# A fused block of five layers on one core: the first mixer begins with the pooling branch, contraction outermost, and the norm's affine part moves behind the spatial product

## What is computed

```python
mod = silu(c) @ ada_w[l] + ada_b[l]              # 1024 -> 3072
shift, scale, gate = jnp.split(mod, 3, axis=-1)
h = x * (1.0 + scale) + shift
proj = h @ w_in                                  # 1024 -> 5120
u, v, z_a, x_b, z_b = split(proj)                # 1024 each
# spatial unit: 4 heads of 256 features, blocks of 128 tokens
v = layer_norm(v per head, norm_g, norm_b)       # norm_g, norm_b: 256
sv = einsum('hts,bnshd->bnthd', masked ws, v) + bs.T
a = u * sv * silu(z_a)
# pooling: 4 groups of 256, trailing means over 2, 4, 8, 16 tokens, minus the token
y = einsum('bsgd,gde->bsge', pooled(x_b), pool_w)
b = (y + pool_b) * pool_scale * silu(z_b)
y = concat([a, b]) @ w_out
x = layer_norm(ALPHA * x + (1.0 + gate) * y, ln_g, ln_b)
```

## Time and profile before

| | |
|---|---|
| median of 3 runs | 1896.85 us (1893.95 to 1897.05) |
| profiled execution | 1895.36 us |
| its span, first to last instruction | 1893.6 us |
| PE busy | 1815.3 us, 96% |
| DVE, ACT, POOL busy | 819.3, 737.6, 832.9 us |
| mean granted clock of PE | 0.991 of full speed |
| output projection of the first mixer begins | 301.61 us |

### The profile page before, as it was taken

How to read it: one execution, slowest core, us unless ns; L and a number is a source line. 1 busy time by engine, 2 the same in 40 slices (tenths; PEclk the granted TensorE clock), 3 DMA queues, 4 the chain that set the end, 5 groups by cost and what they waited for, 6 DMA issues and landing times.

```text
span 1893.6 us, 24041 instructions
## 1 busy us (share of the span) xinstructions
PE 1815.3 (96%) x8796; PEld 1503.0 (79%) x8796; DVE 819.3 (43%) x1388; ACT 737.6 (39%) x1030; POOL 832.9 (44%) x1033
## 2 busy tenths in 40 slices
PE   5999899989999999899999999999997999999998
PEld 5887778877888878788888888888965788888886
DVE  7478666467767750733151111102678341111102
ACT  2223322265565651422253443313556354344222
POOL 1666565447010153255425555353444135555352
PEclk9999999999999999899999999999999999999999
DMA  9234645422121223134323334322311133333321
GB/s 309 89 112 126 190 162 179 161 63 59 36 72 38 79 100 111 46 91 131 99 80 89 106 93 122 111 89 89 116 57 45 45 90 89 92 108 89 109 102 67
DMA packets 211649, 191.19 MB, mean 101 GB/s; under 512 B 10504, under 2 KB 192891, under 8 KB 211579
## 3 DMA queue, kind: packets, MB, share of 16 engines
q1 hardware_dynamic: 210944, 189.95, 32.5%
q10 hardware_dynamic: 634, 0.29, 0.1%
HBM read 188.12 MB, written 2.10 MB: 100 GB/s over the span
## 4 chain that ended last, share of the span: by engine, by line
PE 85%; DVE 6%; ACT 3%; POOL 2%; issue 2%; DMA 1%; SPq 1%; ACTq 0%; POOLq 0%; DVEq 0%
PE PS L1710 26%; PE PS L1712 26%; PE PS L1711 26%; POOL w_low L610 2%; PE PS L2009 1%; PE PS L1838 1%; ACT w_high L706 1%; PE PS L2040 1%; SPq L436 1%; DVE ada_odd L1099 1%; DMA ada_raw<-in_ada_w 1%; POOL w_low L648 1%; DVE soft L1665 0%; DVE probs L1663 0%; PE PS L2032 0%
## 5 line engine op out<-in xcount | busy, mean ns | idle before, releaser
L610 POOL TENSOR_TENSOR w_low<-w_raw,w_high 128x256 fp32r<-128x256 f32 x949 | 741.7, 819 | 822.7 <-ACT w_high L706 822.6
L1710 PE MATMUL PS<-h_high,w_high 128*128 128x512 f32 (+1 forms) x1488 | 560.9, 377 | 17.0 <-DVE h_low L1343 7.1
L706 ACT ACTIVATE w_high<-w_raw 128x2048 fp32r<-128x2048 f32 (+1 forms) x150 | 281.9, 1880 | 729.1 <-PE PS L1712 693.4
L1711 PE MATMUL PS<-h_low,w_high 128*128 128x512 f32 (+1 forms) x1488 | 555.1, 373 | 0.0
L1712 PE MATMUL PS<-h_high,w_low 128*128 128x512 f32 (+1 forms) x1488 | 554.9, 373 | 0.0
L1710 PEld LDWEIGHTS PS<-h_high,w_high 128*128 128x128 f32 x1488 | 283.1, 190 | 69.4 <-DVE h_low L1343 8.3
L1712 PEld LDWEIGHTS PS<-h_high,w_low 128*128 128x128 f32 x1488 | 282.8, 190 | 48.9
L1711 PEld LDWEIGHTS PS<-h_low,w_high 128*128 128x128 f32 x1488 | 283.3, 190 | 45.7 <-issue 0.5
L1216 DVE TENSOR_TENSOR gate_buf<-gate_buf,PS 128x512 f32<-128x512 f32 x44 | 30.2, 688 | 335.5 <-ACT gate_buf L756 334.8
L1271 DVE TENSOR_TENSOR w_low<-w_raw,w_high 128x2048 fp32r<-128x2048 f32 x11 | 25.2, 2292 | 315.4 <-ACT w_high L706 315.4
L1710 PE MATMUL PS<-w_high,ff_high 128*128 128x512 f32 x352 | 137.3, 390 | 0.1
(11 more groups left out here) (302 smaller groups left out, 2612.4 us busy)
## 6 DMA issues: line engine op xcount, KB each, us to landing
w_raw<-in_f_gate_up SPq DMA_DIRECT2D x88, 512.0 KB, 4.9
w_raw<-in_e_w_in SPq DMA_DIRECT2D x40, 512.0 KB, 4.8
w_raw<-in_f_down SPq DMA_DIRECT2D x40, 512.0 KB, 4.2
gains<-in_ada_w SPq DMA_DIRECT2D x16, 1024.0 KB, 5.2
w_raw<-in_a_w_in SPq DMA_DIRECT2D x24, 512.0 KB, 4.4
w_raw<-in_o_w_in SPq DMA_DIRECT2D x20, 512.0 KB, 4.4
ada_raw<-in_ada_w SPq DMA_DIRECT2D x8, 1024.0 KB, 11.9
w_raw<-in_e_w_out SPq DMA_DIRECT2D x16, 512.0 KB, 6.4
```

The costliest lines, as they stand in the source:

```text
L610: ins = nc.gpsimd.tensor_tensor(WL[s][:, piece], raw[s][:, piece], WH[s][:, piece].bitcast(F32), ALU.subtract)
L706: nact(WH[s][:, 0:n], raw[s][:, 0:n], ACT.Copy).then_inc(w_high[s], 1)
L1710: mm(dst, lh, rh, start=first, stop=False, skip_group_check=True)
L1711: mm(dst, lh, rl, start=False, stop=False, skip_group_check=True)
```

## The change

- The ring's stages `v`, `xb`, `pool` and `zb` become one stage `front` of seven pairs in the order xb (five chunks), zb (four), v (four), pool (one). `zu` comes behind it, directly ahead of `eout`.
- xb's first seven column tiles are made with the contraction outermost: four chunks, each of two k tiles by seven column tiles (896 columns), into seven banks that stay open. The eighth column tile is a chunk of its own of 1024 columns.
- The modulation blocks are loaded and used in the order 0, 4, 1, 5, 2, 6, 3, 7, so that two blocks give shift and scale of two k tiles; after two blocks DVE makes these four columns. Blocks 2 to 7 are turned into columns between the matmuls of xb.
- x is transposed by feature tiles into banks 0 to 7; ACT evicts it, tiles 0 and 1 with scale and shift, the others as they are, and modulates them later from SBUF. DVE takes the low parts of h and of the first four weight chunks.
- The affine part of the norm is applied behind the spatial product: norm_g as a scale of the output's partitions, norm_b times the row sums of the masked weights (one more product, by a matrix of ones) in the bias.
- The pooling's rounding and low parts are done by groups, on ACT and DVE. Its product is evicted by ACT into `yb`, silu(z_b) is kept in `zs`, their product comes later (`pool_gate`).
- Positions 0 to 3 of the later modulation blocks are used up in `front`, 4 to 11 in `zu`.

The core of the diff:

```diff
 RING = [
-    ("v", 2, (2, 2)),
-    ("xb", 2, (2, 2)),
+    ("front", 7, (2, 2)),
     ("zu", 4, (2, 2)),
-    ("pool", 1, (2, 2)),
-    ("zb", 2, (2, 2)),
...
+ADA_ORDER = (0, 4, 1, 5, 2, 6, 3, 7)
+XB_TILES = 7
+XB_DEEP = XB_TILES * P
+FRONT_SIZE = [2 * XB_DEEP] * 4 + [K * P] + [CHUNK] * 9
+ZB_AT, V_AT, POOL_AT = 5, 9, 13
...
# SP
+            first_ada(0)
+            first_ada(1)
+            load_xb(0)
             for t in range(T):
                 sp.dma_start(x[:, t, :], ...)
+            for j in range(1, 4):
+                first_ada(2 * j)
+                first_ada(2 * j + 1)
+                load_xb(j)
...
+            load_zb(0)
+            sp.wait_ge(hx_low, K)
             ada_load(0)
+            load_zb(1)
+            ada_load(1)
+            load_zb(2)
+            load_zb(3)
+            ada_load(2)
+            load_v(0)
+            ada_load(3)
+            load_v(1)
+            ada_load(4)
+            load_v(2)
+            load_v(3)
...
+            for c in range(8):
                 load_zu(c)
+                if c >= 2:
+                    ada_load(c + 3)
+                if c == 3:
+                    sp.wait_ge(sv_ready, K)
+                    gate_load(0)
...
# ACT
+            for j in range(1, 4):
+                front_high(j)
+                modulated(2 * j)
+                modulated(2 * j + 1)
+            front_high(4)
+            front_high(ZB_AT)
...
+            for f in range(K):
+                xb_out(f)
+            front_high(ZB_AT + 1)
+            for q in range(4):
+                if q < 3:
+                    pooled_high(q)
+                zb_gate(q)
+                front_high(ZB_AT + 2 + q)
+            pooled_high(3)
+            front_high(V_AT + 2)
+            front_high(V_AT + 3)
+            v_root(0)
+            front_high(POOL_AT)
+            front_high(POOL_AT + 1)
+            for f in range(3):
+                pool_out(f)
+            v_root(1)
+            for f in range(3, K):
+                pool_out(f)
+            zb_high(0)
+            zb_high(1)
+            front_high(POOL_AT + 2)
+            for f in range(2, K):
+                zb_high(f)
...
# DVE
+            for j in range(4):
+                first_terms(2 * j)
+                first_terms(2 * j + 1)
+                split_low("front", j // 2, j % 2, FRONT_SIZE[j])
+                dve.wait_ge(ada_done, 2 * j + 2)
+                v.tensor_tensor(of_step(mod[:, 0:2 * K], j), of_step(PS[:, 7, 256:256 + 2 * K], j), ..., ALU.add).then_inc(mod_ready, 1)
+                for kt in (2 * j, 2 * j + 1):
+                    dve.wait_ge(hx_high, kt + 1)
+                    v.tensor_tensor(hL[:, kt, :], h_tmp[kt % 4], hH[:, kt, :].bitcast(F32), ALU.subtract).then_inc(hx_low, 1)
...
+            def spatial(f):
+                h, m = f // 2, f % 2
+                steps.link(v.scalar_tensor_tensor(sv_bias[m], ws_sum[:, h, :], b_col, bs_bc[:, h * P:(h + 1) * P], ALU.mult, ALU.add))
+                dve.wait_ge(sp_done, f + 1)
+                v.scalar_tensor_tensor(sv[:, f, :]..., PS[:, f, :]..., g_col, sv_bias[m]..., ALU.mult, ALU.add).then_inc(sv_ready, 1)
...
+            ada_terms(0)
+            dve.wait_ge(w_high[1], BASE["front"].split[1] + ZB_AT // 2 + 1)
+            h = CHUNK // 2
+            v.tensor_tensor(WL[1][:, 0:h], ...).then_inc(front_dve, 1)
+            pool_rows(0)
+            pool_rows(1)
+            ada_terms(1)
+            pool_rows(2)
+            pool_rows(3)
+            pooled_low(0)
+            rest_columns()
+            ada_terms(2)
+            pool_rows(4)
+            pool_rows(5)
+            pooled_low(1)
+            dve.wait_ge(sum_done, 1)
+            v.tensor_copy(ws_sum, ...).then_inc(ws_sums, 1)
+            pool_rows(6)
+            pool_rows(7)
+            ada_terms(3)
+            pooled_low(2)
+            pooled_low(3)
+            gate_norm(0)
+            gate_norm(1)
...
+            pool_gate(0)
+            for f in range(K):
+                spatial(f)
+            for f in range(2, K, 2):
+                pool_gate(f)
...
# PE
+            first_column(0)
+            first_column(1)
...
+            for kt in range(K):
+                j, s = kt // 2, kt // 2 % 2
+                if kt % 2 == 0:
+                    front_split(j)
+                pe.wait_ge(hx_low, kt + 1)
+                for f in range(XB_TILES):
+                    if kt == 0:
+                        pe.wait_ge(xt_free, f + 1)
+                    c = slice((kt % 2) * XB_DEEP + f * P, (kt % 2) * XB_DEEP + (f + 1) * P)
+                    ins = mm3(PS[:, f, :], WH[s][:, c], WL[s][:, c], hH[:, kt, :], hL[:, kt, :], kt == 0, kt == K - 1)
...
+                    if kt % 2 and f == 3 and kt < K - 1:
+                        first_column(kt + 2)
+                if kt % 2 == 0 and kt < K - 2:
...
+                    first_column(kt + 2)
```

More of the change, by code:

```diff
@@ L592, in _ @@
             pool.sem_inc(ada_sum, CREDIT)
+            for first_layer in (tr_done, h_high, h_ready, mod_half):
+                pool.sem_inc(first_layer, T)
             def turn_queries(g):
@@ new lines, in _, with xb_out @@
+            front_high(0)
+            modulated(0)
+            modulated(1)
+            for kt in range(2, K):
+                x_turned(kt)
+            for j in range(1, 4):
[4 more added lines that the diff above has]
+            front_high(ZB_AT)
+            def xb_out(f):
+                if f < XB_TILES - 1:
+                    act.wait_ge(xb_done, f + 1)
+                elif f == XB_TILES - 1:
+                    act.wait_ge(used[1], BASE["front"].use[1] + 2)
+                else:
+                    act.wait_ge(used[0], BASE["front"].use[0] + 3)
+                nact(xbufs[f][:, PAD:], PS[:, f, :], ACT.Copy).then_inc(xb_ready, 1)
@@ new lines, in zb_gate, with pooled_high, v_root @@
+            def zb_gate(q):
+                s = (ZB_AT + q) % 2
+                act.wait_ge(used[s], BASE["front"].use[s] + (ZB_AT + q) // 2 + 1)
+                for m in range(2):
+                    nact(zs[:, 2 * q + m, :], PS[:, 2 * (q % 2) + m, :], ACT.Silu).then_inc(zs_ready, 1)
+            def pooled_high(g):
+                act.wait_ge(pooled_ready, 2 * g + 2)
+                nact(poolH[:, 2 * g:2 * g + 2, :], pooled[:, 2 * g:2 * g + 2, :], ACT.Copy).then_inc(pool_high, 1)
+            def v_root(n):
@@ L1130, in low_mod @@
                                 ALU.subtract).then_inc(h_ready, 1)
[L1132 to L1149 removed]
+            v.memset(ones[:, :], 1.0).then_inc(ones_ready, 1)
@@ new lines, in _, with pool_rows @@
+            for z in (*xbufs, sum_a, sum_b):
+                ins = v.memset(z[:, 0:PAD], 0.0)
+            steps.link(ins)
+            def pool_rows(f):
+                g = f // 2
+                win = POOL_WINDOWS[g]
+                dve.wait_ge(xb_ready, f + 1)
+                cur, step, nxt = xbufs[f], 1, [sum_a, sum_b]
+                while step < win:
+                    dst = nxt[0]
+                    nxt.reverse()
+                    steps.link(v.tensor_tensor(dst[:, PAD:], cur[:, PAD:], cur[:, PAD - step:PAD + S - step], ALU.add))
+                    cur, step = dst, 2 * step
+                steps.link(v.scalar_tensor_tensor(pooled[:, f, :], cur[:, PAD:], 1.0 / win, xbufs[f][:, PAD:], ALU.mult, ALU.subtract))
+                head = pooled[:, f, 0:PAD]
+                steps.link(v.tensor_tensor(head, cur[:, PAD:2 * PAD], inv_count[:, g * PAD:(g + 1) * PAD], ALU.mult))
+                v.tensor_tensor(head, head, xbufs[f][:, PAD:2 * PAD], ALU.subtract).then_inc(pooled_ready, 1)
@@ L1876, in _ @@
                     ins.then_inc(ws_tr, 1)
-                pe.wait_ge(w_split[s], B.split[s] + n + 1)
+                if q == 1:
+                    pe.wait_ge(wT_ready, 1)
+                    pe.wait_ge(ones_ready, 1)
+                    mm(PS[:, 7, :], ones[:, :], wT.rearrange("p h t -> p (h t)"), start=True, stop=True).then_inc(sum_done, 1)
+            for q in range(4):
+                n, s = q // 2, (V_AT + q) % 2
+                front_split(V_AT + q)
                 for t in range(T):
-                    if c == 0:
-                        pe.wait_ge(h_ready, t + 1)
-                    if c == 2 and t == 2:
-                        pe.wait_ge(wT_ready, 1)
+                    if q == 0 and t == 2:
+                        pe.wait_ge(ws_sums, 1)
+                    if q == 2:
+                        pe.wait_ge(zs_ready, 6 if t < 2 else 8)
@@ L1899, in _ @@
+            for f in range(K):
+                if f == 0:
+                    pe.wait_ge(vn_ready, 2)
+                if f >= 4:
+                    pe.wait_ge(yb_ready, f + 1)
                 for b in range(T):
-                    ins = mm(PS[:, SIDE[f], b * P:(b + 1) * P], vn[:, b, f * P:(f + 1) * P], wT[:, f // 2, :], start=True, stop=True)
+                    ins = mm(PS[:, f, b * P:(b + 1) * P], vn[:, b, f * P:(f + 1) * P], wT[:, f // 2, :], start=True, stop=True)
```

(3 more changed lines are left out.)

435 lines of the change are left out of this document (202 added, 233 removed).

## The result

The changed kernel took 1877.94 us (median of 4 runs, 1876.41 to 1878.75), the kernel before 1896.93 beside it: a ratio of 0.9903, 95% interval 0.9885 to 0.992, faster by 19.0 us. Measured again beside later experiments it took 1876.54 (ratio 0.9889, 0.9874 to 0.9905). The profiled execution took 1876.41 us (span 1874.3), 18.95 less than that of before; I compare these two.

A forecast was written before the change was run, and what follows sets the result against it. TensorE at its matmuls was taken to bound the kernel (85% of the span). Gains of 13.3 (opening) and 0.8 (middle), 14.1 us, took 1895.4 to 1881.3, as a median 1882.8, stated as 1882.5; range 1873 to 1894.

The forecast's parts named there:

- The opening: Start through the first 192 matmuls: PE starts at about 22 instead of 41.6, ends at 73.3 instead of 86.6; gain 13.3.
- The steps were right: Each two-k-tile step of xb: 9.5 us of matmuls, 2.0 for two columns, 0.6 of wait, 12.1 in all.
- The middle: From the first 192 matmuls to the output projection: new costs of 13.9 against 14.7 us of old losses; gain 0.8.
- (c): In zu, PE waits for four spatial evictions behind a pair of pool gates: 0.8 us.
- (d): Six more pool gates on ACT ahead of zu's first gate, its third weight split behind them: 2.5 us, ends 1 and 8.
- (a): In zb and v, ACT's rounding of pooled waits for DVE ahead of v's first weight split: 3 us allowed, ends 0 and 21.
- (b): SP's queue: modulation block 4 waits for DVE's fourth set of terms, v's third weight chunk stands behind it: 1.0 us.
- (e): Before the output stage: zu's last gate precedes the last modulation column on DVE; wait of 3.69 plus 2.4 of clock: 6.1.
- The steps ran at the full clock: Rival judged: xb's three step waits would bring half clock, 7.2 us more, 1889.7; chance 0.08.
- The waits don't come: Rival: (a) to (d) fall away in the middle, 7.3 us less, freed DVE gives more, down to 1873; chance 0.13.
- slower: Rival: DVE stays beside POOL throughout, 45 us, so v's first and third chunks come late: 1901.3; chance 0.10.

The follow-up runs named there:

- e7: Kernel before, with the low part of pooled done by four DVE operations ahead of zu's loop instead of one POOL operation: 1896.4 us, ratio 1.0.
- e9: Kernel before, with DVE forming the terms of modulation block 0 ahead of the last two rows of trailing sums: 1902.08 us, ratio 1.0022.
- e12: Kernel before, pooled's rounding moved behind zu's second tile, POOL's low part divided over four chunks, three ACT table loads removed: 1887.1 us, ratio 0.9944.
- e2: Changed kernel, with DVE taking the last two pairs of modulation columns before zu's last gate, not behind it: 1872.86 us, ratio 0.9871.
- e3: Changed kernel, with the norm's affine part back on DVE behind the norm, without row sums and scaled eviction: 1881.71 us, ratio 0.9916.
- e5: Changed kernel, with all eight modulation blocks loaded and made into columns before x is transposed, none between matmuls: 1885.72 us, ratio 0.9943.
- e4: Changed kernel, with the low part of pooled again one POOL operation by v's third weight chunk, instead of four on DVE: 1879.33 us, ratio 0.9911.
- e11: Kernel before, with ACT's rounding of pooled moved behind zu's second tile and three ACT table loads removed: 1894.63 us, ratio 0.9984.

## Why the prediction was right, and where its steps were off

The time came out 4.6 us under the forecast of 1882.5, inside the range. In part that is luck: the opening gave 1.9 less than forecast and the middle 6.4 more. The steps:

**The opening.** Predicted gain 13.3, measured 11.4. The start was at 23.95 for 22: it is this term that was low, by 1.95 us. I let the last x tile (19.2) set it, and PE's own work did: the second column of the pair stood at 15.01, the 32 transposes followed it without a gap and took 6 us (16.73 to 22.67), not 5.1, and the handovers over ACT and DVE 1.28 more. The steps were right: 12.1 predicted, 12.07 measured, and so were their parts, read from starts as I had priced them. A column moved the stream by 0.91 (the second matmul behind it is at 29.93 where the pace puts it at 29.02), for 2 x 0.46. The first matmul of a step stands 0.54 later than the pace and the next one 0.08 more, for 0.6; the 0.38 that the profile gives as idle is less, since a matmul's record is longer than its distance to the next.

**The middle.** Predicted gain 0.8, measured 7.2: this is the step that failed. Of the 6.4 us 2.1 are a loss in the kernel before that I priced too low, and 4.3 are waits that I charged to the changed kernel and that didn't come. To the first: I wrote "The stage zu takes 96.6 us for 384 matmuls (87.2) and seven columns of 0.46 (3.2): 6.2 us lost." There are three columns in that stage, at 210.74, 222.13 and 233.51, since positions 0 to 3 are for the gate and are kept as sums. From the first matmul of zu (137.24) to the last of these columns 96.27 us pass: less 87.05 and two columns of 0.46, zu lost 8.3, not 6.2. In the changed kernel it is 90.69 (184.91 to 275.60), less 87.05 and six columns, 0.9. So zu alone gave 7.4, as much as the whole middle; the rest of it (a first wait in zb, one more product, the two ends) comes out near even.

What it lost, read from starts, was 1.6 us at the wait of 1.29, 4.0 at that of 2.39 (1.5 of them at the low clock, seven matmuls from 184.99 on; the granted clock was 0.50 from 184.9 to 188.0) and 2.5 at that of 2.19. I named the POOL operation as standing in it, and had no price for what it did to the others. e7 showed that giving it to DVE inside zu doesn't help, and e9 that forming the first terms earlier doesn't when the sums come later for it. With the rounding later and the low part in four pieces, e12's zu loses 0.2 us (88.19 to its last column, less 87.05 and two columns) where the kernel before lost 8.3. The change does both between zb and v, by groups, and its zu loses 0.9. That this is the same 8 us is argued from the two traces; no run puts the operations back inside zu in the changed kernel. (c) and (d) I had put at 0.8 and 2.5, as if zu kept losing; a late spatial eviction cost 0.58 and zu's third split 0.33.

**The other terms.** (a) 3 us for DVE late at v: DVE was done with rows 4 and 5 at 108.6, before ACT needed them, and PE didn't wait at v; it waited 0.27 before zb's last chunk (111.62), whose low part took POOL 9.0 beside DVE. The 1.52 at the first zb chunk I hadn't listed. (b) 1.0 for SP's queue: nothing. (e) 6.1 for the end: 3.74 of waiting, and 1.7 of clock in this trace, 2.3 in the second one of the same kernel (from the wait's end to the third matmul of the output projection 4.37 and 5.04, in e2 2.70); e2 got back 4.6 in the trace, 5.1 in the medians. "This work was hidden before … and is worth nothing" is true of the affine part in the old order; e3 shows that it is worth 3.8 in the new one, which a reader who undoes parts one by one must know.

**The rivals.** The steps ran at the full clock: 0.38 us of waiting at a step cost none. The Trainium skill's rule ("TensorE: Matmul & The Clock Gate", section "HAM oscillation"), that a loop which waits at every k tile throttles again, isn't borne out by waits of this size; the page's own case waits 3 to 5 us at each k tile. "The waits don't come" was mostly true: of the 7.3 us of (a) to (d) 2.7 were seen (1.52 + 0.27, 0, 0.58, 0.33), so 4.6 fell away. The wait that "slower" names came when DVE was given 8 more operations, at v's first chunk.

**Of the 19 us**, then: 8 to 10 from feeding the first projection as the modulation arrives (e5, by the ratios), and about as much from no longer having `pooled`'s rounding and low part in one piece each inside zu (e12, on the kernel before: 8.6 in the first mixer of the trace, 10.6 in the medians). The two are measured from opposite ends and add up to about the whole, which fits the account and doesn't prove it. The affine part's move keeps 3.8 of the gain.

## What to carry to other kernels

A large operation that rounds or splits a finished tensor belongs where its engine has idle time before the next chunk, in pieces no longer than that idle time. In one piece it held ACT's and POOL's weight splits and one operation of DVE, and through SP's queue a load two chunks on. Where the chunks around it had room, at v in e4, POOL's operation in one piece cost no more than 1.4 to 2.8 us. When a stage loses time, count its instructions from rows before pricing its loss. And a gain that looks like the change's headline (the earlier start) may be half of it: undo the headline alone and see what stays.

## What was unexpected of the hardware

The length of a wait doesn't say what the clock does behind it. Waits of 2.39 and 2.32 us (e11, at 252.22: the first matmul took 0.77, and the granted clock was 0.50 until 255) brought the low clock. One of 2.19 didn't, and neither did one of 2.36 in the kernel before (clock 1.00 from 253.4 to 256), though it is longer than e11's at the same place:

```profile
253.49 0.47 PE L1710 MATMUL PS<-h_high,w_high 128*128 128x512 f32 x1 [2.36 <-issue]
253.80 0.40 PE L1711 MATMUL PS<-h_low,w_high 128*128 128x512 f32 x1
```

And the drop can come late: of the waits of 3.6 to 3.7 us before the pooling product the one of 3.69 had it at the first matmul, that of e12 only from the fourth, at 230.54, 0.8 us after PE had gone on (granted clock 0.97 up to 230.5, 0.50 from there to 233). PE's timeline of e12 shows it:

```profile
230.05 0.39 PE L1721 MATMUL PS<-pool_low,w_high 128*128 128x512 f32 x1
230.28 0.46 PE L1722 MATMUL PS<-pool_high,w_low 128*128 128x512 f32 x1
230.54 0.63 PE L1720 MATMUL PS<-pool_high,w_high 128*128 128x512 f32 x1
230.96 0.63 PE L1721 MATMUL PS<-pool_low,w_high 128*128 128x512 f32 x1
```

So "the first matmul took 0.5" isn't the sign that a wait was free of it; the starts of the next ten must be read.

DVE's timeline of e12 beside POOL's operation at 168.49:

```profile
168.52 2.65 DVE L1109 SCALAR_TENSOR_TENSOR ada_odd<-gains,csil,ada_odd 128x256 f32<-128x256 f32 x1
171.09 0.47 DVE L1109 SCALAR_TENSOR_TENSOR gate_sum<-gains,csil,gate_sum 128x256 f32<-128x256 f32 x1
```

A POOL operation of 1024 columns beside a DVE operation with two SBUF inputs held that one for 2.6 us (DVE at 168.52 and at 180.09 in e12), its own length, as the one of 4096 held it for 9.27: the hold goes by the length of the other engine's single operation, and eight instructions of 256 columns in a row let DVE in between, at 0.95 for 0.47 us.
